# Probability times values in head pairs: values as the stationary operand, two heads side by side in one PSUM bank, rows no longer transposed a second time

## Chip, core and metric

One NeuronCore of one Trainium2 chip runs the whole program. The metric is the device time of one execution in microseconds (us). The engines are TensorE (PE, and PEld for its weight loads), VectorE (DVE), ScalarE (ACT), GpSimd (POOL) and SyncE (SP, which issues most transfers).

## The reference

Six transformer layers for 256 tokens of width 1024. The change touches the softmax attention in five of them. With `h` heads of 64 features, each head computes

```python
sc = jnp.einsum('bkgqd,bksd->bkgqs', qg, k) * scale        # (+ bias, window or causal mask)
o = jnp.einsum('bkgqs,bksd->bkgqd', jax.nn.softmax(sc, axis=-1), v)
mix = jnp.concatenate([merge_heads(a_out), merge_heads(b_out), merge_heads(c_out), merge_heads(d_out)], axis=-1)
mix = jnp.einsum('bse,ed->bsd', mix, w_o[l])
```

- Two layers of the first block (called MIX here) have 20 softmax items each: 8 of differential attention, which come in pairs that are subtracted from one another and then normalised, and 12 plain ones (4 grouped-query, 4 neighbourhood, 4 latent heads), not causal: 256 queries by 256 keys.
- Two layers of the second block (SWA, with a sink logit and a window) and one (FOX, with a forget gate) have 16 plain, causal items each. The fourth (GLA) has no softmax.

So there are 16 items of the differential kind and 24 + 32 + 16 = 72 plain ones.

## The kernel before

Weights come in units of 128 x 2048 through three buffers `raw`. ACT rounds each into `whi` (`act_hi`, L885), DVE makes the rest `wlo` (`dve_lo`, L894), and each product is three matmuls (hi x hi, hi x lo, lo x hi). These matmuls fill nearly all the time of PE.

Attention is laid into slots between quarters of such units, by the tables `MIX`, `SWA` and `FOX` of class `Plan`. In each slot every engine does, in its own fixed order, a part of several items. An item k whose scores are made in slot h is transposed in slot h+2 and valued in slot h+3.

- PE: a quarter of a unit; transposes of the probabilities of an item into bank `pso` (L737), scores (L751); then `pe_value` (L766); then, where the table has a turn, `pe_turn` (L612). In slots where the plan is `joint`, the scores of two heads stand together in the even slot: their 64 features lie in the upper and the lower half of the partitions, and their results go to two banks.
- ACT: the copy of the transposed probabilities to `probT` (L796), the exponentials with their row sums (L810), the rounding of a turned column block to `ahi` (L645), and `act_hi`.
- DVE: the masked scores and their maxima (L846 or L840), then `dve_divide` (L819 to L828), then `alo` (L649), then other work of the slot, such as rotary embeddings, `dve_lo`, and products for the modulation.

An item's output is tokens by features: `probT` is stationary (128 x 128), the 64 value features move, and there are 4 matmuls of 64 columns, or 3 if causal. DVE divides by the row sums and writes 128 x 64 blocks into `rows`. The output projection wants features by tokens, so when two heads are ready, `pe_turn` transposes their 128 columns back and ACT and DVE split them into `ahi` and `alo`.

The semaphores that order it are `s_done` (scores), `max_ready`, `p_ready` (exponentials), `t_done` (transposes), `pt_ready` (copy), `o_done` (values), `o_evac` (divided). `prob` has two buffers, and the mask of item k waits for the transposes of item k-2, since both use one of them.

Of the kernel before, what the change touches and what calls it, by code (L numbers as in the profile page):

```python
# [113 lines left out]
def build(nc, wts, ada, ada_b, x_in, c_row, rel_bias, col1, row1, gain_mix, gain_ffn, col2, row2,  # L114
# [4 lines left out]
    with ctx:  # L119
# [77 lines left out]
        prob, probT = fold(w(8000, 1024), 2, 512), fold(w(9024, 1024), 2, 512)  # L197
# [62 lines left out]
        o_evac = sem("o_evac")  # L260
        mix_ready = sem("mix_ready")
# [345 lines left out]
        def pe_turn(pe, g, m, bank=1):  # L607

            if not isinstance(m, int) or m > 0:
                pe.wait_ge(m_lo, 8 * g + m)  # L610
# [29 lines left out]
        def act_turn(act, l, c, m, g, bank=1):  # L640

            act.wait_ge(m_tr, 8 * g + m + 1)
            if m >= 4:
                act.wait_ge(unit_mm, unit_no(l, c) + m // 2 - 1)
            nc.scalar.copy(ahi[:, m % 4], psu[:, bank, 0:SEQ]).then_inc(m_hi, 1)  # L645

        def dve_turn(dve, m, g, bank=1):
            dve.wait_ge(m_hi, 8 * g + m + 1)
            nc.vector.tensor_tensor(alo[:, m % 4], psu[:, bank, 0:SEQ], ahi[:, m % 4].bitcast(f32), ALU.subtract).then_inc(m_lo, 1)  # L649
# [77 lines left out]

        def pe_begin(pe, I0, items, plan, h):
# [3 lines left out]
            if k is not None:  # L732
                pe.wait_ge(p_ready, I0 + k + 1)
                if k >= 1:
                    pe.wait_ge(pt_ready, I0 + k)
                for _, _, at in blocks(items[k]):
                    last = nc.tensor.transpose(pso[:, at:at + P], prob[:, k % 2, at:at + P], ident[:])  # L737
# [18 lines left out]
        def pe_value(pe, I0, items, plan, h):  # L756
            k = plan.value(h)
            if k is not None:
                it = items[k]
                pe.wait_ge(pt_ready, I0 + k + 1)  # L760
                if k >= 1:
                    pe.wait_ge(o_evac, I0 + k)
                if it["vpre"] is not None:
                    pe.wait_ge(*it["vpre"])
                for t, kc, at in blocks(it):
                    last = mm(psm[:, t * HD:(t + 1) * HD], probT[:, k % 2, at:at + P],  # L766
                              it["v"][kc], start=(kc == 0), stop=(kc == 1 or at == P))
                last.then_inc(o_done, 1)

        def pe_mix_turn(pe, I0, plan, h, g):  # L770


            m = plan.turn.get(h)
            if m is not None:
                pe.wait_ge(o_evac, I0 + 2 * m + 2)
                pe_turn(pe, g, m)

        def pe_mix1_turn(pe, l, I0, h):
# [3 lines left out]
            if m is not None:  # L782
                if m < 2:
                    pe.wait_ge(mix_ready, l + 1)
                else:
                    pe.wait_ge(o_evac, I0 + 2 * m + 6)
                pe_turn(pe, l, m)

        def act_copy(act, I0, items, plan, h):
            k = plan.transpose(h)  # L790
            if k is not None:
                act.wait_ge(t_done, I0 + k + 1)
                if k >= 2:
                    act.wait_ge(o_done, I0 + k - 1)
# [1541 lines left out]
```

## Time and profile before

| | |
|---|---|
| median of 3 runs | 1897.2 us (1896.7 to 1898.39) |
| the profiled execution: its time, its span | 1897.12 us, 1895.1 us |
| PE, PEld, DVE, ACT, POOL busy, share of the span | 98%, 90%, 71%, 50%, 4% |
| granted clock of TensorE, mean | 0.998 |
| all value matmuls (L766), x608 records, busy | 80.9 us |
| all transposes of probabilities (L737), x304, busy | 47.6 us |
| all transposes of rows (L612), x96, busy | 18.7 us |
| exponentials (L810), x144, busy with their form's mean 463 ns | 66.5 us |

Each float32 matmul shows as two records, a transpose and an fp32r matmul as one. Records of matmuls overlap, so the time that a group takes is read from its start to the start of the group behind it, not from the sum of the durations. Windows are in us from the start of the span. The attention stages lie at 56 to 135 and 386 to 465 (MIX), 698 to 762 and 1631 to 1695 (SWA) and 1322 to 1408 (FOX).

### The profile page before, as it was taken

How to read it: one execution, taken by the hardware profiler on the slowest of the kernel's cores; microseconds unless marked ns; L12 is line 12 of the kernel's file. 1: busy time of each engine (PE TensorE's matmuls, PEld its weight loads, DVE VectorE, ACT ScalarE, POOL GpSimd, SP SyncE). 2: the span in 40 equal slices, each digit the busy share in tenths (PEclk: the TensorE clock that was granted, in tenths of full speed). 3: DMA queues.
4: the chain of work that ended last, by engine and by line, in shares of the span. 5: the costliest groups of instructions: out<-in, count | busy, mean ns of one | idle time of the engine just before them, and what ended most of it. 6: DMA issues, size and time to landing. Idle time of an engine off the chain costs nothing.

```text
span 1895.1 us, 34211 instructions
## 1 busy us (share of the span) xinstructions
PE 1855.8 (98%) x13368; PEld 1702.6 (90%) x13368; DVE 1354.9 (71%) x2194; ACT 953.2 (50%) x1470; POOL 77.0 (4%) x98
## 2 busy tenths in 40 slices
PE   8999999999999999999999999999999999999998
PEld 8989999998999987899989799998989998979997
DVE  6758888775878877888877587886555556766555
ACT  7755334766533466533473553345654334664333
POOL 3003000000000000000000000003300000000000
PEclk9999999999999999999999999999999999999999
DMA  8538987533788742788854388875335554335552
GB/s 305 188 125 259 353 307 304 190 134 134 290 329 307 297 177 97 262 326 308 315 198 139 119 300 323 306 279 225 122 138 190 192 181 165 132 113 199 189 187 89
DMA packets 62060, 416.60 MB, mean 220 GB/s; under 512 B 9008, under 2 KB 9200, under 8 KB 13312
## 3 DMA queue, kind: packets, MB, share of 16 engines
q1 hardware_dynamic: 56016, 401.33, 57.4%
q0 software_dynamic: 5936, 13.79, 2.6%
q8 instruction: 72, 1.18, 0.2%
q14 instruction: 36, 0.29, 0.0%
HBM read 413.90 MB, written 3.19 MB: 220 GB/s over the span
## 4 chain that ended last, share of the span: by engine, by line
PE 89%; DVE 6%; ACT 2%; issue 1%; DVEq 1%; ACTq 0%; DMA 0%; SPq 0%
PE psu L524 35%; PE psy L692 18%; PE psy L586 7%; PE psy L578 5%; PE psy L632 5%; PE psu L541 4%; PE psm L766 3%; PE psy L565 2%; PE psu L751 2%; PE pso L737 1%; PE psy L655 1%; DVE x L1164 1%; DVE wlo L894 1%; PE psy L1680 1%; DVEq L1163 1%
## 5 line engine op out<-in xcount | busy, mean ns | idle before, releaser
L885 ACT CAST whi<-raw 128x2048 fp32r<-128x2048 f32 (+1 forms) x281 | 536.2, 1908 | 599.1 <-PE psu L524 396.4
L894 DVE TENSOR_TENSOR wlo<-raw,whi 128x2048 fp32r<-128x2048 f32 (+5 forms) x306 | 646.6, 2114 | 257.2 <-ACT whi L885 256.5
L524 PE MATMUL psu<-hlo,whi 128*128 128x256 f32 x1920 | 536.0, 279 | 0.0
L524 PE MATMUL psu<-hhi,whi 128*128 128x256 f32 x1920 | 535.9, 279 | 0.0
L524 PE MATMUL psu<-hhi,wlo 128*128 128x256 f32 x1920 | 535.8, 279 | 0.0
L524 PEld LDWEIGHTS psu<-hhi,whi 128*128 128x128 f32 x1920 | 360.8, 188 | 2.3
L524 PEld LDWEIGHTS psu<-hlo,whi 128*128 128x128 f32 x1920 | 360.8, 188 | 2.3
L524 PEld LDWEIGHTS psu<-hhi,wlo 128*128 128x128 f32 x1920 | 360.8, 188 | 0.0
L1096 DVE CUSTOM_DVE_ANT_0 ada_raw<-ada_raw,cvec 128x1024 f32<-128x1024 f32 x192 | 227.0, 1220 | 2.2 <-DMA ada_raw<-ada 2.2
L692 PE MATMUL psy<-whi,ahi 128*128 128x512 f32 x528 | 210.2, 398 | 0.0
L692 PE MATMUL psy<-wlo,ahi 128*128 128x512 f32 x528 | 207.9, 394 | 0.0
L692 PE MATMUL psy<-whi,alo 128*128 128x512 f32 x528 | 207.4, 393 | 0.0
L586 PE MATMUL psy<-whi,hhi 128*128 128x256 f32 x448 | 131.4, 293 | 0.0
L586 PE MATMUL psy<-wlo,hhi 128*128 128x256 f32 x448 | 125.9, 281 | 0.0
L586 PE MATMUL psy<-whi,hlo 128*128 128x256 f32 x448 | 125.8, 281 | 0.0
L692 PEld LDWEIGHTS psy<-wlo,ahi 128*128 128x128 f32 x528 | 99.1, 188 | 25.4
L692 PEld LDWEIGHTS psy<-whi,alo 128*128 128x128 f32 x528 | 99.1, 188 | 21.0
L692 PEld LDWEIGHTS psy<-whi,ahi 128*128 128x128 f32 x528 | 99.1, 188 | 20.5
L586 PEld LDWEIGHTS psy<-whi,hhi 128*128 128x128 f32 x448 | 84.5, 189 | 4.9 <-issue 4.8
L766 PEld LDWEIGHTS psm<-work 128*128 128x128 f32 x608 | 76.1, 191 | 13.5 <-issue 7.2
L810 ACT ACTIVATE work<-work,nmax 128x256 f32<-128x256 f32 (+1 forms) x144 | 66.5, 463 | 40.9 <-DVE nmax L846 40.9
L586 PEld LDWEIGHTS psy<-whi,hlo 128*128 128x128 f32 x448 | 84.6, 189 | 0.1
(337 smaller groups left out, 2981.2 us busy)
## 6 DMA issues: line engine op xcount, KB each, us to landing
raw<-wts SPq DMA_DIRECT2D x280, 1024.0 KB, 4.8
ada_raw<-ada SPq DMA_DIRECT2D x96, 1024.0 KB, 5.0
gain<-gate_rows POOLq DMA_DIRECT2D x8, 512.0 KB, 3.9
dense_bias<-rel_bias POOLq DMA_DIRECT2D x32, 64.0 KB, 10.1
nab<-dense_bias SPq DMA_DIRECT2D x2, 1024.0 KB, 7.1
ada_raw<-fox_rows POOLq DMA_DIRECT2D x4, 512.0 KB, 13.3
cb<-cst POOLq DMA_DIRECT2D x1, 1408.0 KB, 8.2
cb<-cst SPq DMA_DIRECT2D x1, 1056.0 KB, 10.1
```

Of the source, the lines that this page charges most:

```text
L524: last = mm(psu[:, bank, cc * SEQ:(cc + 1) * SEQ], a[:, cols], h[:, kt, :], start=(kt == 0 and j == 0), stop=(kt == KT - 1 and j == 2))
L541: last = mm(psu[:, banks[u], cc * SEQ:(cc + 1) * SEQ], a[:, cols], h[:, kt, :], start=(kt == 0 and cc == 0 and j == 0), stop=(kt == KT - 1 ...
L565: last = mm(psy[:, j, half * width:(half + 1) * width], h[:, kt, toks], a[:, kt * width:(kt + 1) * width], start=start, stop=stop, skip_gr ...
L578: last = mm(o, a[:, cols], h[:, kt, :], start=(kt == 0 and j == 0), stop=(kt == KT - 1 and j == 2))
L586: last = mm(o, h[:, kt, toks], a[:, kt * width:(kt + 1) * width], start=(kt == 0 and j == 0), stop=(kt == KT - 1 and j == 2))
L632: last = mm(psy[:, 2 * t + half, :], h[:, (2 * s + ff) % 4, toks], b[:, cols], start=(s == 0 and ff == 0 and j == 0), stop=(s == 3 and ff ...
L692: last = mm(psy[:, 2 * t + half, :], h[:, aslot + ff, toks], b[:, cols], start=(first_step and ff == 0 and j == 0), stop=(last_step and ff ...
L766: last = mm(psm[:, t * HD:(t + 1) * HD], probT[:, k % 2, at:at + P], it["v"][kc], start=(kc == 0), stop=(kc == 1 or at == P))
L810: last = nc.scalar.activation(prob[:, k % 2, span], src[:, span], ACT.Exp, bias=nmax[:, k % 4, t:t + 1], scale=1.0 if plain else -1.0, acc ...
L885: nc.scalar.copy(whi[:, part_of(c), 0:n], raw[:, slot_of(c), 0:n]).then_inc(hi_done, 1)
L894: last = nc.vector.tensor_tensor(wlo[:, part_of(c), cols], raw[:, slot_of(c), cols], whi[:, part_of(c), cols].bitcast(f32), ALU.subtract)
L1096: last = nc.vector.tensor_tensor_reduce(tile, tile, cvec[:], 1.0, 0.0, ALU.mult, ALU.add, ada_part[:, 2 * half + j:2 * half + j + 1])
```

## The change

The 16 differential items stay as they are. For the 72 plain items:

- The exponentials are normalised before the transposes. DVE makes the reciprocals one slot after the scores (`dve_roots`, first in its slot), and ACT multiplies the probabilities in place, two activations per item (`act_normal`, between the copy and the exponentials of a slot). The transposes wait for that (`pn_ready`) instead of for the exponentials.
- Nothing is valued at the even item. At the odd one, the values of both heads are stationary (128 x 64 each) and `probT` moves, 256 columns at a time. The two heads' results lie in partitions 0 to 63 and 64 to 127 of one bank, features by tokens. `probT` gets a third buffer, and its two key halves are laid so that a head's 256 queries lie in one row.
- DVE copies the 128 x 256 result once per pair (`dve_divide`), and ACT and DVE make `ahi` and `alo` from the copy. `pe_turn` stays only for the differential heads (two per MIX layer) and for GLA.

```diff
-        prob, probT = fold(w(8000, 1024), 2, 512), fold(w(9024, 1024), 2, 512)
+        prob, probT = fold(w(8000, 1024), 2, 512), fold(w(9024, 1536), 3, 512)
...
             if k is not None:
-                pe.wait_ge(p_ready, I0 + k + 1)
+                if items[k]["pair"] is None:
+                    pe.wait_ge(pn_ready, plain_no(I0, items, k) + 1)
+                else:
+                    pe.wait_ge(p_ready, I0 + k + 1)
                 if k >= 1:
                     pe.wait_ge(pt_ready, I0 + k)
...
                 it = items[k]
+                if it["pair"] is None and k % 2 == 0:
+                    return
                 pe.wait_ge(pt_ready, I0 + k + 1)
...
+                if it["pair"] is None:
+                    for kc in range(2):
+                        for i in (k - 1, k):
+                            toks, at = (slice(kc * P, SEQ), P + kc * SEQ) if it["causal"] else (slice(0, SEQ), kc * SEQ)
+                            last = mm(psm[HD * (i % 2):HD * (i % 2) + HD, toks], items[i]["v"][kc],
+                                      probT[:, i % 3, at:at + toks.stop - toks.start], start=(kc == 0), stop=(kc == 1))
+                    last.then_inc(o_done, 2)
+                    return
...
+        def act_normal(act, I0, items, plan, h):
+            k = plan.score(h - 1)
+            if k is not None and items[k]["pair"] is None:
+                act.wait_ge(r_ready, plain_no(I0, items, k) + 1)
+                for t, span in enumerate(spans(items[k])):
+                    last = nc.scalar.activation(prob[:, k % 2, span], prob[:, k % 2, span], ACT.Copy, scale=rsum[:, k % 4, t:t + 1])
+                last.then_inc(pn_ready, 1)
+
+        def dve_roots(dve, I0, items, plan, h):
+            k = plan.score(h - 1)
+            if k is not None and items[k]["pair"] is None:
+                dve.wait_ge(p_ready, I0 + k + 1)
+                if items[k]["sink"] is not None:
+                    nc.vector.tensor_tensor(psum_[:, k % 4], psum_[:, k % 4], esink[:, k % 4], ALU.add)
+                    nc.vector.drain()
+                nc.vector.reciprocal(rsum[:, k % 4], psum_[:, k % 4]).then_inc(r_ready, 1)
...
+            if it["pair"] is None:
+                if k % 2 == 1:
+                    dve.wait_ge(o_done, I0 + k + 1)
+                    m = k // 2 - (2 if plan is MIX else 0)
+                    nc.vector.tensor_copy(columns(plan, m), psm[:, 0:SEQ]).then_inc(o_evac, 2)
+                return
...
-                pe_mix_turn(pe, I0, SWA, h, g)
...
                 act_copy(act, I0, items, SWA, h)
+                act_normal(act, I0, items, SWA, h)
...
-                    act_turn(act, DEPTH1, c0 + 6, SWA.turn[h], g)
+                    m = SWA.turn[h]
+                    act_turn(act, DEPTH1, c0 + 6, m, g, columns(SWA, m), o_evac, I0 + 2 * m + 2)
```

On PE, in an SWA layer where a slot takes one quarter of the output projection (L632, in the new program L634), from the end of one slot to the end of the next. Before:

```order
L766 MATMUL psm<-work 128x64 x3
L612 MATMUL psu<-ident,rows 128x128 x2
L632 MATMUL psy<-whi,ahi 128x512
L632 MATMUL psy<-whi,alo 128x512
L632 MATMUL psy<-wlo,ahi 128x512
L632 MATMUL psy<-whi,ahi 128x512
L632 MATMUL psy<-whi,alo 128x512
L632 MATMUL psy<-wlo,ahi 128x512
L737 MATMUL pso<-ident,work 128x128 x3
L751 MATMUL psu<-work 128x128
L751 MATMUL psu<-work 128x256
L766 MATMUL psm<-work 128x64 x3
```

Now, the same place (L759 are the transposes, L773 the scores, L793 the values):

```order
L759 MATMUL pso<-ident,work 128x128 x3
L634 MATMUL psy<-whi,ahi 128x512
L634 MATMUL psy<-whi,alo 128x512
L634 MATMUL psy<-wlo,ahi 128x512
L634 MATMUL psy<-whi,ahi 128x512
L634 MATMUL psy<-whi,alo 128x512
L634 MATMUL psy<-wlo,ahi 128x512
L759 MATMUL pso<-ident,work 128x128 x3
L773 MATMUL psu<-work 128x128
L773 MATMUL psu<-work 128x256
L793 MATMUL psm<-work 64x256 x2
L793 MATMUL psm<-work 64x128 x2
```

The two groups of three narrow matmuls and the two transposes of rows are gone, and four wider ones stand at the end of every second slot, each with 64 output partitions.

On ACT, one slot of an SWA layer that holds an evacuation (L1742), a column block to round (L645) and a weight unit (L885). Before:

```order
L1742 ACTIVATE work<-psy 128x512
L796 COPY work<-pso 128x384
L808 ACTIVATE esink<-nmax,prow 128x2
L810 ACTIVATE work,psum_<-work,nmax 128x128
L810 ACTIVATE work,psum_<-work,nmax 128x256
L645 CAST ahi<-psu 128x256
L885 CAST whi<-raw 128x2048
```

Now:

```order
L1794 ACTIVATE work<-psy 128x512
L817 COPY work<-pso 128x384
L843 ACTIVATE work<-work,rsum 128x128
L843 ACTIVATE work<-work,rsum 128x256
L829 ACTIVATE esink<-nmax,prow 128x2
L831 ACTIVATE work,psum_<-work,nmax 128x128
L831 ACTIVATE work,psum_<-work,nmax 128x256
L647 CAST ahi<-rows 128x256
L934 CAST whi<-raw 128x2048
```

Two activations have come in ahead of the exponentials, and the rounding reads SBUF instead of PSUM.

On DVE, a slot with an odd item in the joint part of an SWA layer. Before:

```order
L846 ISA work,nmax<-psy,cb,nsink 128x128
L846 ISA nmax 128x1
L846 ISA work,nmax<-psy,cb,nsink 128x256
L846 ISA nmax 128x1
L819 TENSOR_TENSOR psum_<-psum_,esink 128x2
L821 RECIPROCAL rsum<-psum_ 128x2
L828 TENSOR_TENSOR rows<-psm,rsum 128x2x64
L649 TENSOR_TENSOR alo<-psu,ahi 128x256
L894 TENSOR_TENSOR wlo<-raw,whi 128x1024
```

Now:

```order
L853 TENSOR_TENSOR psum_<-psum_,esink 128x2
L855 RECIPROCAL rsum<-psum_ 128x2
L893 ISA work,nmax<-psy,cb,nsink 128x128
L893 ISA nmax 128x1
L893 ISA work,nmax<-psy,cb,nsink 128x256
L893 ISA nmax 128x1
L651 TENSOR_TENSOR alo<-rows,ahi 128x256
L943 TENSOR_TENSOR wlo<-raw,whi 128x1024
```

The sum and the reciprocal moved ahead of the mask, where they wait for ACT's exponentials of the slot before; the division is gone.

## Rows read from the trace of the kernel before

**Rows 1.** The page: busy time by engine; the chain that ended last, by engine.

```profile
PE 1855.8 (98%) x13368; PEld 1702.6 (90%) x13368; DVE 1354.9 (71%) x2194; ACT 953.2 (50%) x1470; POOL 77.0 (4%) x98
...
PE 89%; DVE 6%; ACT 2%; issue 1%; DVEq 1%; ACTq 0%; DMA 0%; SPq 0%
```

**Rows 2.** Busy time in windows of four slots: two of SWA, one of MIX.

```profile
core 0: us, PE busy (x) PEld busy (x) DVE busy (x) ACT busy (x) POOL busy (x), PEclk, DMA share, GB/s
1641.99:1654.66 12.67, 12.67 (x111) 11.60 (x110) 7.86 (x33) 9.46 (x29) 0.00 (x0) 1.00 0.20 77
1654.66:1668.42 13.76, 13.21 (x89) 10.56 (x88) 10.53 (x37) 9.48 (x29) 0.00 (x0) 1.00 0.21 77
101.13:116.63 15.50, 15.50 (x95) 12.89 (x93) 9.14 (x27) 8.96 (x25) 0.00 (x0) 1.00 0.28 101
```

**Rows 3.** Timeline of PE in MIX: start, length, engine, line, operation, count.

```profile
92.11 1.00 PE L766 MATMUL psm<-work 128*128 128x64 f32 x8
92.92 0.36 PE L586 MATMUL psy<-whi,hhi 128*128 128x256 f32 x1
...
94.97 0.48 PE L751 MATMUL psu<-work 64*128 64x256 f32 x1
94.97 0.48 PE L751 MATMUL psy<-work 64*128 64x256 f32 x1
...
96.03 1.10 PE L766 MATMUL psm<-work 128*128 128x64 f32 x8
96.97 0.39 PE L612 MATMUL psu<-ident,rows 128*128 128x128 f32 x2
```

**Rows 4.** Timeline of PE in SWA: slots 10 and 11.

```profile
1640.45 0.37 PE L751 MATMUL psu<-work 64*128 64x128 f32 x1
...
1641.30 0.88 PE L766 MATMUL psm<-work 128*128 128x64 f32 x6
1641.99 0.36 PE L586 MATMUL psy<-whi,hhi 128*128 128x256 f32 x1
...
1643.83 0.78 PE L766 MATMUL psm<-work 128*128 128x64 f32 x6
1644.45 0.39 PE L612 MATMUL psu<-ident,rows 128*128 128x128 f32 x2
1644.59 0.36 PE L586 MATMUL psy<-whi,hhi 128*128 128x256 f32 x1
```

**Rows 5.** Timeline of PE in FOX: values after a quarter.

```profile
1343.23 0.78 PE L766 MATMUL psm<-work 128*128 128x64 f32 x6
1343.82 0.37 PE L578 MATMUL psy<-hhi,whi 128*128 128x256 f32 x1
```

**Rows 6.** Timeline of ACT in SWA, slot 10 and the copy of slot 11.

```profile
1642.20 0.30 ACT L808 ACTIVATE esink<-nmax,prow 128x2 f32<-128x2 f32 x1 [1.17 <-DVE nmax L846]
1642.40 0.39 ACT L810 ACTIVATE work<-work,nmax 128x128 f32<-128x128 f32 x1
1642.70 0.19 ACT L810 ACTIVATION_READ_ACCUMULATOR work<-work,nmax 128x1 f32 x1
1642.79 0.49 ACT L810 ACTIVATE work<-work,nmax 128x256 f32<-128x256 f32 x1
1643.19 0.19 ACT L810 ACTIVATION_READ_ACCUMULATOR work<-work,nmax 128x1 f32 x1
...
1644.19 0.47 ACT L796 COPY work<-pso 128x384 f32<-128x384 f32 x1
```

**Rows 7.** Timeline of DVE in SWA, slot 10.

```profile
1641.40 0.35 DVE L846 CUSTOM_DVE_ANT_0 work<-psu,cb,nsink 128x128 f32<-128x128 f32 x1 [0.59 <-PE psy L751]
...
1642.22 0.16 DVE L819 TENSOR_TENSOR psum_<-psum_,esink 128x2 f32<-128x2 f32 x1
1642.46 0.17 DVE L821 RECIPROCAL rsum<-psum_ 128x2 f32<-128x2 f32 x1
```

**Rows 8.** The longest kind of wait in SWA, 1631 to 1695: us in total, times, longest.

```profile
ACT esink L808 <- DVE nmax L846: 12.6, 10, 2.0
```

More of the change, by code:

```diff
@@ L726, in blocks, with turned_at, columns, plain_no @@
                 (t, kc, t * SEQ + kc * P) for t in range(NT) for kc in range(2)]
+        def turned_at(it, t, kc, at):
+            return at if it["causal"] or it["pair"] is not None else kc * SEQ + t * P
+        def columns(plan, m):
+            at = 256 if plan is MIX and m == 4 else m * SEQ
+            return scratch[:, at:at + SEQ]
+        def plain_no(I0, items, k):
+            before = sum(it["pair"] is None for it in items[:k])
+            return I0 - 8 * min(I0 // 20, DEPTH1) + before
         def pe_begin(pe, I0, items, plan, h):
@@ L732, in pe_begin @@
             if k is not None:
-                pe.wait_ge(p_ready, I0 + k + 1)
+                if items[k]["pair"] is None:
+                    pe.wait_ge(pn_ready, plain_no(I0, items, k) + 1)
+                else:
+                    pe.wait_ge(p_ready, I0 + k + 1)
                 if k >= 1:
                     pe.wait_ge(pt_ready, I0 + k)
-                for _, _, at in blocks(items[k]):
-                    last = nc.tensor.transpose(pso[:, at:at + P], prob[:, k % 2, at:at + P], ident[:])
+                for t, kc, at in blocks(items[k]):
+                    to = turned_at(items[k], t, kc, at)
+                    last = nc.tensor.transpose(pso[:, to:to + P], prob[:, k % 2, at:at + P], ident[:])
                 last.then_inc(t_done, 1)
@@ L869, in dve_steps @@
             if h in plan.turn:
-                dve_turn(dve, plan.turn[h], g)
+                m = plan.turn[h]
+                dve_turn(dve, m, g, psu[:, 1, 0:SEQ] if plan is MIX and m < 2 else columns(plan, m))
         def act_hi(act, l, c, i=0, first=False):
@@ L1329, in act_mix1 @@
                 act_copy(act, I0, items, MIX, h)
+                act_normal(act, I0, items, MIX, h)
                 act_exp(act, I0, items, MIX, h)
@@ L1374, in act_mix1 @@
                 if h in MIX.turn:
-                    act_turn(act, l, C1_O, MIX.turn[h], l)
+                    m = MIX.turn[h]
+                    if m < 2:
+                        act_turn(act, l, C1_O, m, l, psu[:, 1, 0:SEQ], m_tr, 2 * l + m + 1)
+                    else:
+                        act_turn(act, l, C1_O, m, l, columns(MIX, m), o_evac, I0 + 2 * m + 6)
                 if h == 33:
@@ L1775, in act_fox @@
                 act_copy(act, I0, items, FOX, h)
+                act_normal(act, I0, items, FOX, h)
                 act_exp(act, I0, items, FOX, h)
@@ L1788, in act_fox @@
                 if h in FOX.turn:
-                    act_turn(act, DEPTH1, c0 + 13, FOX.turn[h], g)
+                    m = FOX.turn[h]
+                    act_turn(act, DEPTH1, c0 + 13, m, g, columns(FOX, m), o_evac, I0 + 2 * m + 2)
                 if h == 28:
@@ L1883, in act_gla @@
                 if h in GLA.turn:
-                    act_turn(act, DEPTH1, c0 + 13, GLA.turn[h], g, 0)
+                    act_turn(act, DEPTH1, c0 + 13, GLA.turn[h], g, psu[:, 0, 0:SEQ], m_tr, 2 * DEPTH1 + GLA.turn[h] + 1)
                 if h == 57:
@@ L1990, in dve_gla @@
                 if h in GLA.turn:
-                    dve_turn(dve, GLA.turn[h], g, 0)
+                    dve_turn(dve, GLA.turn[h], g, psu[:, 0, 0:SEQ])
                 if h in (4, 40):
```

48 lines of the change are left out of this document (20 added, 28 removed).

## The prediction

> **What bounds the kernel now.** I read the page first: PE is busy for 98% of the span and holds 89% of the chain that ended last, DVE 71% and 6%, ACT 50% and 2% [rows 1]. So a microsecond taken out of PE's stream comes out of the time, as long as another engine does not take its place. Whether one does is not told by a mean over the span, so I then read windows of four slots inside the stages that change [rows 2]. PE is busy nearly throughout at the full granted clock (1.00, the 2.4 GHz level) in all three. ACT is busy 9.46 of 12.67 us in the first half of SWA, 9.48 of 13.76 in the second, 8.96 of 15.50 in MIX; DVE 7.86, 10.53 and 9.14. That is the room into which the change puts work. Last I read PE's timeline for what a value group takes, from its start to the next group's [rows 3 to 5].
>
> **What leaves PE.** A value group of a plain item in MIX takes 92.92 - 92.11 = 0.81 us alone, and 96.97 - 96.03 = 0.94 right behind scores [rows 3]. In SWA it takes 1641.99 - 1641.30 = 0.69 behind scores and 1644.45 - 1643.83 = 0.62 otherwise, and the two transposes of rows behind it 0.14 [rows 4]. In FOX it takes 1343.82 - 1343.23 = 0.59 [rows 5]. Two items and one turn make a pair: 0.94 + 0.81 + 0.14 = 1.89 us in MIX, 0.69 + 0.62 + 0.14 = 1.45 in SWA, 0.59 + 0.59 + 0.14 = 1.32 in FOX.
>
> **What comes into PE.** No row shows a matmul with 64 output partitions beside another. The nearest rows are the joint scores: two heads in two halves of the array, by rows of the array instead of by columns. Their records in `psu` and `psy` start together at 94.97, and the whole of them (per half four records of 256 columns) takes 96.03 - 94.97 = 1.06 us [rows 3]. The causal form (per half two records of 128 columns and two of 256) takes 1641.30 - 1640.45 = 0.85 [rows 4]. The new value group has the same records per half: two key blocks, each float32 and so two records, of 256 columns without a mask, of 256 and 128 with it. If its halves run side by side, it takes 1.06 and 0.85. These prices hold the cost of leaving the split array, and 28 of the 36 groups stand in slots with scores or late in their stage, mostly right behind scores, where the array was split already (by rows, not by columns: no row shows what that change costs, and I take nothing, with 0.1 apiece, 2.8 us, as the other end). In FOX a quarter lies between, so I add the 0.1 by which a group changed in length beside a split one (0.94 against 0.81) [rows 3]: 0.95.
>
> If the halves run one after the other, the streaming comes twice. The two forms differ by 2 x 128 columns and by 1.06 - 0.85 = 0.21 us, so a record of 256 columns streams for 0.21, four of them for 0.84 and the causal four for 0.63; the rest, 0.22, is switching. A group then takes 1.90 and 1.48, and 1.58 in FOX. These are the two ends. I take the first, since the nearest row has two halves of this same array side by side in float32 at just this length.
>
> - MIX: 6 pairs in each of 2 layers, 12 x (1.89 - 1.06) = 10.0 us less.
> - SWA: 8 pairs in each of 2 layers, 16 x (1.45 - 0.85) = 9.6 us less.
> - FOX: 8 pairs, 8 x (1.32 - 0.95) = 3.0 us less.
>
> Together 22.6 us, if nothing else holds PE.
>
> **What comes into ACT.** Two activations per plain item. An activation of this kind, SBUF to SBUF with a scale per partition, is nearest to the exponentials: 1642.70 - 1642.40 = 0.30 us for 128 columns and 1643.19 - 1642.79 = 0.40 for 256 [rows 6]. So an SWA or FOX item costs 0.70 and a MIX item 0.80 (bounds: 0.39 and 0.49 apiece if nothing overlaps). ACT loses nothing; the rounding to `ahi` only reads another place. Four slots then ask of ACT [rows 2]:
>
> - SWA, first half: 9.46 + 4 x 0.70 = 12.26 us, where PE wants 12.67 - 2 x 0.60 = 11.47. ACT is now the longer one.
> - SWA, second half: 9.48 + 2.80 = 12.28, where PE wants 13.76 - 1.20 = 12.56. ACT fills 98% of it.
> - MIX: 8.96 + 4 x 0.80 = 12.16, where PE wants 15.50 - 2 x 0.83 = 13.84: 88%.
>
> This is where gain is given back. In the first half of SWA (three pairs) I count all of it as lost, 3 x 0.60 = 1.8 us a layer: 0.8 a window by the sums above, and the rest because ACT's load comes in lumps (weight units) and it waits for DVE, 12.6 us in ten waits in the last SWA stage [rows 8], not all of which can go. In the second half I count half of three pairs, 0.9; the last two pairs, behind the last scores, keep all. That is 2.7 a layer, 5.4 us for both. For MIX I take 0.5 a layer, 1.0 together, for FOX nothing.
>
> **The new ring.** DVE's reciprocals now stand first in its slot and wait for the exponentials of the slot before; mask and maxima stand behind them, and ACT's next exponentials wait for these. Round the ring: the exponentials with their sums 1643.19 + 0.19 - 1642.20 = 1.18 us [rows 6], sum and start of the reciprocal some 0.3, mask and maxima from 1641.40 until ACT starts at 1642.20, 0.80 [rows 6, 7]. That is 2.3 us, with hand-overs 2.4, for a slot of 12.67 / 4 = 3.2 (2.9 after the change). So the ring alone does not bind. Behind the blocked reciprocal on DVE are the mask, the copy of values, the rest `alo` that the output projection waits for, and `dve_lo`, which PE's next weight unit waits for; a half-unit of `dve_lo` in the slot ahead makes the reciprocal late, then the normalising, then PE's transposes. Between one slot's transposes and the next's, ACT needs only copy and normalising, 0.4 + 0.7, so some 1.8 us of lateness are free.
>
> **What leaves DVE.** A pair had two divisions and now has one copy of 128 x 256. The two turns of `psu` on PE no longer wait for DVE. DVE gets no longer in any window, and where it is busiest (10.53 of 13.76) it is not the longest. I count nothing.
>
> **Sum.** 1897.1 (the profiled execution, whose span is 1895.1, and which lies 0.1 from the median) - 22.6 + 5.4 + 1.0 = 1880.9. The two givings-back are the least certain, and lean to more rather than less: I say 1882.
>
> **The rivals.** A measurement of this kernel can tell about 0.2%, 3.8 us, from no change.
>
> 1. *Side by side, a part given back in SWA* (forecast, 0.71): 1874 to 1889. At the low end ACT's work is absorbed everywhere (22.6 less), at the high end SWA gains nothing and MIX gives back 3.
> 2. *The halves run one after the other* (0.13). The joint scores differ in that each half reads other rows of the array; here both halves take all 128 rows, and two streams must enter at once. What would decide it is that the second head's matmuls start when the first's end. Then MIX gets 12 x (1.89 - 1.90) = -0.1 us, SWA 16 x (1.45 - 1.48) = -0.5, FOX 8 x (1.32 - 1.58) = -2.1: 2.7 longer. With the 2.8 for the change from a row split to a column split it is 1897.1 + 5.5 = 1903, slower. PE is then long enough to hide ACT.
>    The Trainium skill, "TensorE: Matmul & The Clock Gate", Part 3, says that weight loads run beside matmuls in flight only where the row groups differ, which here they don't; by it each load would stand bare between the matmuls. By that rule this rival would hold. The trace does not agree for the full array: the eight loads and matmuls of a value group, all in the same row group, take 0.81 us [rows 3]. The same part says that three column tiles gained 2.38 times, which speaks for the first case; no run here shows it yet.
> 3. *ACT and DVE set the pace of all the stages* (0.16). Speaking for it: 98% and over 100% in SWA, and the ring. Against it: 88% in MIX. If each slot of SWA's 14 with scores or transposes became 0.5 us longer than PE wants, by DVE's other work falling into the ring, that is 14 us for both layers; with 2 in MIX and 1 in FOX it leaves 22.6 - 17 = 5.6: 1891.5, from 1888 to 1899.
>
> **How the numbers follow.** The time is that of the first case. Faster by over 0.2% (under 1893.4): the first case and over a third of the third, 0.77. Within 0.2%: the rest of the third and a little of the second, 0.11. Slower: 0.12. The range leaves out less than a tenth below 1874 and over a tenth above 1898; the first case's own is 1874 to 1889.
>
> **What would show it.** Side by side: the records of L793 start in twos, and a group takes 1.06 or 0.85. The normalising: L843 at 0.30 and 0.40 apiece. In SWA: ACT over 95% busy from slot 9 to 19, and PE's transposes (L759) idle ahead for ACT, by 0.5 to 1 us after each weight unit; in MIX and FOX hardly. Wrong would make it: a value group near 1.9 (second case), PE idle in every slot, or an activation with a scale per partition that costs more than the exponentials.

## The result and the profile after

The changed kernel takes 1914.4 us (median of 4 runs, 1910.9 to 1915.14) against 1897.5 us before (4 runs beside it, 1896.7 to 1898.39). The ratio is 1.0086, 95% interval [1.007, 1.0102]: slower, by less than 1% but clear of the noise. The forecast was 1882.0 us, from 1874 to 1898. The profiled execution took 1915.1 us, its span is 1913.4.

The page of the changed kernel, busy time by engine and the chain by engine, against [rows 1]:

```profile
PE 1845.7 (96%) x13104; PEld 1665.3 (87%) x13104; DVE 1346.5 (70%) x2158; ACT 1006.6 (53%) x1614; POOL 78.1 (4%) x98
...
PE 84%; DVE 7%; ACT 5%; issue 2%; DVEq 1%; ACTq 1%; DMA 0%; SPq 0%
```

PE works 10.1 us less, and yet the span is 18.3 us longer. PE no longer works without a break: its part of the chain fell from 89% to 84%, and ACT's rose from 2% to 5%. To see where, read the five attention stages as windows, in the order MIX, MIX, SWA, FOX, SWA, each from its normalisation to the start of the feed-forward part behind it. Before:

```profile
core 0: us, PE busy (x) PEld busy (x) DVE busy (x) ACT busy (x) POOL busy (x), PEclk, DMA share, GB/s
8.30:146.10 137.80, 136.51 (x1006) 123.66 (x1004) 95.36 (x208) 96.49 (x204) 16.56 (x22) 1.00 0.58 200
338.90:476.40 137.50, 135.74 (x1005) 122.52 (x1005) 92.58 (x207) 90.81 (x200) 0.61 (x2) 1.00 0.38 142
669.30:765.40 96.10, 93.70 (x660) 81.95 (x660) 70.74 (x186) 61.60 (x150) 2.25 (x5) 0.98 0.37 131
1283.20:1411.30 128.10, 124.91 (x954) 114.05 (x954) 72.43 (x150) 74.78 (x148) 32.73 (x27) 1.00 0.44 161
1602.40:1697.80 95.40, 92.00 (x661) 80.59 (x661) 67.27 (x179) 63.01 (x153) 1.07 (x2) 1.00 0.33 116
```

And after:

```profile
8.20:149.80 141.60, 134.35 (x945) 115.74 (x943) 93.69 (x202) 106.16 (x228) 16.57 (x22) 0.99 0.56 195
342.60:484.20 141.60, 133.53 (x945) 114.48 (x945) 91.03 (x201) 100.51 (x224) 0.65 (x2) 0.99 0.37 138
677.00:781.30 104.30, 94.02 (x612) 76.07 (x612) 69.84 (x178) 73.28 (x182) 2.29 (x5) 0.93 0.34 123
1299.00:1423.10 124.10, 120.81 (x906) 106.12 (x906) 69.75 (x142) 85.83 (x180) 33.78 (x27) 1.00 0.46 166
1614.30:1716.00 101.70, 90.08 (x612) 73.08 (x612) 66.08 (x171) 74.30 (x185) 1.07 (x2) 0.98 0.31 109
```

These windows hold the whole difference. Their lengths sum to 594.9 us before and 613.3 after, 18.4 more; FOX is 4.0 shorter, MIX 7.9 longer in two layers, SWA 14.5 longer in two. Three terms make this up:

- Length less PE's busy time is PE's idle time: 12.1 us before, 40.5 after, **28.5 more**. FOX has none of it (3.2 and 3.3).
- A stage's length times what its mean granted clock lacks of 1.00 is at most what the clock took: 1.4 + 1.4 + 7.3 + 2.0 = 12.1 us after, 1.9 before, **up to 10 more**.
- What is left, 18.4 - 28.5 - 10.2 = **-20.3 us**, is the work that left PE's stream, if the clock took all of that. The forecast was 22.6.

So matmul work left PE's stream about as forecast, and nearly twice of it was given back. Who holds PE is seen in the group of the transposes over the whole program (idle time ahead of it behind the second bar; it was 0.1 us before the change):

```profile
L759 PE MATMUL pso<-ident,work 128*128 128x128 f32 x304 | 49.7, 280 | 20.6 <-ACT work L843 20.5
```

And in the waits of the last SWA stage, 1640 to 1712 (us in total, times, longest):

```profile
DVE alo L651 <- ACT ahi L647: 12.4, 7, 2.2
ACT work L843 <- DVE rsum L855: 8.2, 7, 1.6
PEld pso L759 <- ACT work L843: 7.8, 10, 1.6
PE pso L759 <- ACT work L843: 5.2, 7, 1.2
```

PE waits for ACT's normalising, ACT for DVE's reciprocal, and DVE, ahead of that reciprocal, for ACT's rounding `ahi`. One turn of this ring, on the timeline of the same stage, DVE first, then ACT, then PE:

```profile
1667.44 0.43 DVE L651 TENSOR_TENSOR alo<-rows,ahi 128x256 fp32r<-128x256 f32 x1 [1.76 <-ACT ahi L647]
1667.78 1.22 DVE L943 TENSOR_TENSOR wlo<-raw,whi 128x1024 fp32r<-128x1024 f32 x1
1668.91 0.15 DVE L853 TENSOR_TENSOR psum_<-psum_,esink 128x2 f32<-128x2 f32 x1
1669.14 0.17 DVE L855 RECIPROCAL rsum<-psum_ 128x2 f32<-128x2 f32 x1
```

```profile
1666.92 0.19 ACT L831 ACTIVATION_READ_ACCUMULATOR work<-work,nmax 128x1 f32 x1
1667.01 0.39 ACT L647 CAST ahi<-rows 128x256 fp32r<-128x256 f32 x1
1667.30 0.47 ACT L817 COPY work<-pso 128x384 f32<-128x384 f32 x1
1669.34 0.80 ACT L843 ACTIVATE work<-work,rsum 128x128 f32<-128x128 f32 x2 [1.56 <-DVE rsum L855]
```

```profile
1669.64 0.28 PE L588 MATMUL psy<-wlo,hhi 128*128 128x256 f32 x1
1670.20 0.55 PE L759 MATMUL pso<-ident,work 128*128 128x128 f32 x3 [0.28 <-ACT work L843]
```

The exponentials and their sums are done at 1667.11. The reciprocal needs 0.17 us and starts at 1669.14, two microseconds later: DVE sat 1.76 us for `ahi`, which ACT makes behind the same exponentials, and then did 1.22 us of a weight unit. ACT idles 1.56 us, and the transposes start late; PE had other work to do meanwhile and idles only 0.28 us. No engine is short of time here; each waits for a small piece that stands behind another engine's large one. Where PE has less work left to cover the lateness, it idles longer. In MIX two products of 1.22 us stand ahead of the reciprocal (L1145, from 85.14 on), and PE idles 0.86 us:

```profile
87.69 0.15 DVE L855 RECIPROCAL rsum<-psum_ 128x2 f32<-128x2 f32 x1
87.88 0.91 ACT L843 ACTIVATE work<-work,rsum 128x256 f32<-128x256 f32 x2 [1.54 <-DVE rsum L855]
88.84 0.66 PE L759 MATMUL pso<-ident,work 128*128 128x128 f32 x4 [0.86 <-ACT work L843]
```

There is a second way from the reciprocal to PE, through what stands behind it on DVE. The reciprocal, and in SWA the sum ahead of it, wait for ACT's exponentials, so the mask of the next item comes late. In each SWA stage one projection quarter is to write into `psy` where the last joint scores stand, and waits until the mask has read them. The longest idle time of PE in the stage comes so, the sum on DVE first:

```profile
1679.64 0.16 DVE L853 TENSOR_TENSOR psum_<-psum_,esink 128x2 f32<-128x2 f32 x1 [1.38 <-ACT work L831]
1680.29 0.48 DVE L893 CUSTOM_DVE_ANT_0 work<-psy,cb,nsink 128x256 f32<-128x256 f32 x1
1680.92 0.77 PE L634 MATMUL psy<-whi,ahi 128*128 128x512 f32 x1 [2.26 <-DVE nmax L893]
```

Over the program the first matmuls of all these quarters (L634) have 7.3 us of idle time ahead of them, 4.5 of it for the mask; the same group (L632) had 1.2 us before.

In the four slots that the prediction took as its SWA example, first and second half [rows 2]:

```profile
1654.46:1668.24 13.78, 12.01 (x99) 9.53 (x97) 7.21 (x29) 11.72 (x36) 0.00 (x0) 1.00 0.19 73
1668.24:1685.95 17.71, 13.64 (x76) 9.52 (x75) 11.47 (x41) 13.08 (x39) 0.00 (x0) 0.90 0.17 61
```

The first took 12.67 before and now 13.78, the second 13.76 and now 17.71. ACT is busy for 85% and 74%, not for over 95%.

The new value group does what was forecast, and a little more. In MIX (98.51 to the turn at 99.52) it takes 1.01 us, in FOX and SWA 0.80; the estimates were 1.06, 0.95 and 0.85:

```profile
98.51 1.08 PE L793 MATMUL psm<-work 128*64 128x256 f32 x8
99.52 0.44 PE L614 MATMUL psu<-ident,rows 128*128 128x128 f32 x2
...
1349.62 0.87 PE L793 MATMUL psm<-work 128*64 128x256 f32 x8
1350.42 0.39 PE L580 MATMUL psy<-hhi,whi 128*128 128x256 f32 x1
```

### The profile page after: what moved, and what is told of

Read it like the earlier page. It is cut to its first block, busy times and chain, and to the rows that moved or that the text cites. A ratio compares the mean times of both kernels' runs of the same rounds, so it can differ in the third digit from the quotient of the medians.

```text
span 1913.4 us, 33683 instructions
## 1 busy us (share of the span) xinstructions
PE 1845.7 (96%) x13104; PEld 1665.3 (87%) x13104; DVE 1346.5 (70%) x2158; ACT 1006.6 (53%) x1614; POOL 78.1 (4%) x98
## 4 chain that ended last, share of the span: by engine, by line
PE 84%; DVE 7%; ACT 5%; issue 2%; DVEq 1%; ACTq 1%; DMA 0%; SPq 0%
PE psu L526 35%; PE psy L694 18%; PE psy L588 6%; PE psy L580 5%; PE psy L634 5%; PE psu L543 4%; PE psy L567 2%; PE psu L773 2%; ACT work L831 2%; PE psy L657 1%; DVE wlo L943 1%; DVE x L1213 1%; PE pso L759 1%; ACT work L843 1%; PE psm L793 1%
## 5 line engine op out<-in xcount | busy, mean ns | idle before, releaser
L1145 DVE CUSTOM_DVE_ANT_0 ada_raw<-ada_raw,cvec 128x1024 f32<-128x1024 f32 x192 | 226.9, 1219 | 2.5 <-DMA ada_raw<-ada 2.5
L694 PE MATMUL psy<-whi,ahi 128*128 128x512 f32 x528 | 210.0, 398 | 0.0
L694 PEld LDWEIGHTS psy<-whi,ahi 128*128 128x128 f32 x528 | 99.1, 188 | 20.6
L634 PE MATMUL psy<-whi,ahi 128*128 128x512 f32 x192 | 84.2, 438 | 7.3 <-DVE nmax L893 4.5
L588 PEld LDWEIGHTS psy<-wlo,hhi 128*128 128x128 f32 x448 | 84.4, 188 | 0.0
## 6 DMA issues: line engine op xcount, KB each, us to landing
dense_bias<-rel_bias POOLq DMA_DIRECT2D x32, 64.0 KB, 10.2
```

Of the source, the lines that this page charges most:

```text
L588: last = mm(o, h[:, kt, toks], a[:, kt * width:(kt + 1) * width], start=(kt == 0 and j == 0), stop=(kt == KT - 1 and j == 2))
L634: last = mm(psy[:, 2 * t + half, :], h[:, (2 * s + ff) % 4, toks], b[:, cols], start=(s == 0 and ff == 0 and j == 0), stop=(s == 3 and ff ...
L694: last = mm(psy[:, 2 * t + half, :], h[:, aslot + ff, toks], b[:, cols], start=(first_step and ff == 0 and j == 0), stop=(last_step and ff ...
L1145: last = nc.vector.tensor_tensor_reduce(tile, tile, cvec[:], 1.0, 0.0, ALU.mult, ALU.add, ada_part[:, 2 * half + j:2 * half + j + 1])
```

## The experiments

Three theories were open. *The ring*: PE waits for the chain of exponentials, reciprocal (DVE) and normalising (ACT). Its first rival: ACT's added 53 us of work alone make it the bound. Its second: the saved matmuls themselves did not come, or came by another mechanism than the two column halves. All times below stand beside runs of the kernel before of 1897.2 to 1897.5 us on the same chip.

**1. No ring at all.** The last line goes in MIX and in FOX in the same way.

```diff
-                if items[k]["pair"] is None:
-                    pe.wait_ge(pn_ready, plain_no(I0, items, k) + 1)
-                else:
-                    pe.wait_ge(p_ready, I0 + k + 1)
+                pe.wait_ge(p_ready, I0 + k + 1)
...
-            dve_roots(dve, I0, items, plan, h)
...
-                act_normal(act, I0, items, SWA, h)
```

> The changed kernel without the normalising: no reciprocals for the plain items on VectorE, no normalising activations on ScalarE, and the transposes wait for the exponentials as before. The plain heads' results are left undivided. What is left of the change is TensorE's part and the single copy per pair. Theory A (the new step reciprocal - normalising - transposes, with VectorE's other work of a slot in it, makes TensorE wait and its clock fall): all of the loss goes and TensorE's saving shows, 1873 to 1880 us, granted clock 0.998 as before. Theory B (the new value groups or the later copies cost TensorE more than the sum says): it stays above 1895 us.

Measured: 1883.2 us (1882.53 to 1884.28), ratio 0.9927 [0.9911, 0.9944]. The stages are 136.4, 134.4, 93.2, 124.2 and 92.7 us, 14.0 less than before; with 22.2 us of idle time against 12.1 and a clock that lacks 1.4 us instead of 1.9, the same sum gives 23.6 us for the work that left the stream. The plain heads' results stay undivided here. The new form without its normalising is worth 14.3 us, 3 less than even the low end of what was expected (the time was to be 1880 at most): PE idles 10.1 us more than before the change though the ring is gone. In MIX the turn of the differential heads waits 4.9 us for DVE's `alo` (0.8 before), in SWA the projection quarters (L634) idle 4.4 us (0.6 before). The 31.2 us up to the changed kernel come with the normalising and its ring.

**2. ACT's part of the ring alone.** Same work on ACT, but by a column of ones, waiting only for its own exponentials; no reciprocals on DVE, and so undivided results again.

```diff
-                act.wait_ge(r_ready, plain_no(I0, items, k) + 1)
+                act.wait_ge(p_ready, I0 + k + 1)
...
-                    last = nc.scalar.activation(prob[:, k % 2, span], prob[:, k % 2, span], ACT.Copy, scale=rsum[:, k % 4, t:t + 1])
+                    last = nc.scalar.activation(prob[:, k % 2, span], prob[:, k % 2, span], ACT.Copy, scale=ones[:, 0:1])
...
-            dve_roots(dve, I0, items, plan, h)
```

> The changed kernel in which ScalarE normalises by a column of ones, waiting only for its own exponentials, and VectorE makes no reciprocals for the plain items: ScalarE has all the added work and the transposes wait for it, but VectorE is out of the loop. The plain heads' results are left undivided. Theory A (VectorE's queue in the loop): most of the loss goes, 1878 to 1888 us. Theory C (my forecast's: ScalarE's added load sets the pace in SWA): the loss in SWA stays, 1900 to 1914 us in all, with ScalarE over 95% busy in the first half of SWA.

Measured: 1894.8 us (1892.02 to 1895.68), ratio 0.9982 [0.9972, 0.9991], between the two expectations. The transposes' group now shows

```profile
L759 PE MATMUL pso<-ident,work 128*128 128x128 f32 x304 | 48.7, 276 | 6.1 <-ACT work L843 5.8
```

ACT's normalising costs 1894.8 - 1883.2 = 11.6 us, the reciprocals on DVE another 1914.4 - 1894.8 = 19.6. DVE's part is the larger one, though it is one instruction of 0.15 to 0.17 us per item, and one more in SWA. The 19.6 us hold three things that this pair of kernels does not separate: ACT waits for the reciprocal, DVE waits for the exponentials ahead of it and is late with what stands behind, and DVE is busy 13.2 us longer over the whole program (1346.5 against 1333.3).

**3. The reciprocals earlier on DVE.** They move from the head of the next slot to the tail of their own, behind the division and ahead of the long pieces:

```diff
-            dve_roots(dve, I0, items, plan, h)
             k = plan.value(h)
...
+            dve_roots(dve, I0, items, plan, h + 1)
             if h in plan.turn:
```

> The changed kernel, complete, with VectorE's reciprocals moved from the start of the next slot to the same slot as the scores, behind the copy of values and ahead of the turned block's rest, the rotary work and the weight units. VectorE then waits there for the exponentials, but none of its long pieces stands between them and the reciprocal. Theory A: most of the loss goes, 1880 to 1892 us. Theory C: nothing changes, 1908 to 1918 us. Theory D (VectorE's waiting for the exponentials delays its own weight units instead): 1895 to 1915 us, with waits of TensorE for wlo in place of those for the normalising.

Measured: 1911.5 us (1909.56 to 1915.89), ratio 1.0079 [1.0063, 1.0096]. The transposes' idle time falls from 20.6 to 9.6 us, and the two MIX stages take 138.1 and 137.7 us, as before the change. ACT's wait for the reciprocal is all but gone (39.5 us in the changed kernel, 2.4 here). But DVE now stands still for ACT's exponentials in nearly every slot, 72.6 us in 63 waits against 16.3 in 16, and its mask is late instead. In the last SWA stage:

```profile
1674.96 0.16 DVE L853 TENSOR_TENSOR psum_<-psum_,esink 128x2 f32<-128x2 f32 x1 [1.42 <-ACT work L831]
1676.25 0.76 PE L634 MATMUL psy<-whi,ahi 128*128 128x512 f32 x1 [2.68 <-DVE nmax L893]
```

That stage takes 104.5 us instead of 101.7, FOX 126.5 instead of 124.1. The time lies in the ranges of both Theory C and Theory D. It is D's mechanism with another end: what PE waits for is the mask and not `wlo`. The wait was moved, not removed.

**4. The same, and ACT's normalising ahead of its copy.**

```diff
-                act_copy(act, I0, items, SWA, h)
                 act_normal(act, I0, items, SWA, h)
+                act_copy(act, I0, items, SWA, h)
```

> As the kernel with early reciprocals, and on ScalarE the normalising stands ahead of the copy in each slot, so that it needn't wait for the slot's transposes. Theory A: as e3 or up to 3 us less. If the copy that now comes 0.7 to 0.8 us later holds up the value groups, it is up to 4 us more than e3.

Measured: 1914.7 us (1913.94 to 1915.77), ratio 1.0093 [1.0076, 1.011]. No better than experiment 3, whose runs overlap with these: the transposes now wait 11.8 us for ACT's copy in place of its normalising.

**5. The reciprocals on GpSimd.** Its queue is empty in MIX and in SWA's attention.

```diff
-            if k is not None and items[k]["pair"] is None:
+            if plan is FOX and k is not None and items[k]["pair"] is None:
...
+                pool.wait_ge(p_ready, I0 + k + 1)
...
+                nc.gpsimd.tensor_tensor(rsum[:, k % 4], psum_[:, k % 4], minus1[:], ALU.pow).then_inc(r_ready, 1)
```

> The changed kernel with the reciprocals of the MIX and SWA heads on GpSimd, whose queue is idle there (as a power of minus one), and only FOX's on DVE. The whole computation is done. Theory (about 20 of the 31 us that the new ring costs come from the reciprocal standing in DVE's queue behind its long pieces): near the kernel whose ACT waits for its own exponentials alone, 1894.8, plus GpSimd's latency: 1893 to 1900 us, with hardly any wait of ACT for the reciprocal that a DVE piece ends. Rival (any further engine in the ring costs a hop that PE cannot afford, and DVE's queue has little to do with it): 1905 to 1915 us.

Measured: 1897.8 us (1896.99 to 1903.32), ratio 1.0002 [0.9992, 1.0011]. This takes back 16.6 of the 19.6 us that hang on the reciprocals, with the whole computation done. GpSimd is slow at it, but no long piece stands ahead:

```profile
1650.56 0.20 POOL L452 TENSOR_TENSOR psum_<-psum_,esink 128x2 f32<-128x2 f32 x1 [1.98 <-ACT work L771]
1650.90 0.89 POOL L454 TENSOR_TENSOR rsum<-psum_,minus 128x2 f32<-128x2 f32 x1
```

Sum and power take 0.20 and 0.69 to 0.89 us where DVE takes 0.15 and 0.17 (spans on this engine are rough). The Trainium skill, "Perfetto Trace Analysis", on optimizing GPSIMD operations, advises to prefer other engines because GpSimd is generally slower. On the operation the trace agrees, four to five times (though a power stands here against a reciprocal); on the kernel it does not: the slower engine gives the shorter time. The profiled execution is the longest of the ten, 1903.3 us, 5.5 above the median, so it shows less than the whole gain. ACT waits 23.9 us for reciprocals in it instead of 39.5, and the transposes idle

```profile
L699 PE MATMUL pso<-ident,work 128*128 128x128 f32 x304 | 49.8, 280 | 15.0 <-ACT work L783 14.8
```

instead of 20.6. The gain stands in MIX, where these idle times fall from 10.0 us to 1.6 in the two layers. In the two SWA layers they rise from 10.5 to 13.4, and the stages take 101.7 and 102.1 us against 104.3 and 101.7. So in this execution a queue of its own for the reciprocals does not free SWA; whether it does in the faster ones, no trace shows.

**6. The ring without the saving.** The kernel before, with reciprocals first in the slot, normalising on ACT and the transposes waiting for it; the divisions become copies.

```diff
-                pe.wait_ge(p_ready, I0 + k + 1)
+                if items[k]["pair"] is None:
+                    pe.wait_ge(pn_ready, plain_no(I0, items, k) + 1)
+                else:
+                    pe.wait_ge(p_ready, I0 + k + 1)
...
+            if it["pair"] is None:
+                nc.vector.tensor_copy(rows[:, :, it["col"]:it["col"] + HD], fold(psm[:, 0:P], NT, HD)).then_inc(o_evac, 1)
+                return
```

> The kernel before with the new ring alone: DVE makes the reciprocals first in the slot after the scores, ACT normalises in place, PE's transposes wait for that, and DVE's division of each plain head becomes a copy of the 128x128 result. PE does the same work as before. The whole computation is done. Theory (the ring itself costs what the profile after shows as idle PE, about 27 us of idle and up to 10 us of halved clock, whatever PE does besides): about 1897 + 25 to 35 = 1922 to 1932 us, with the SWA stages and the MIX stages longer by 5 to 9 us each and idle time before the transposes. Rival (PE waits only since its own stream became shorter; with the old stream of 22 us more the same chain fits): below 1907 us.

Measured: 1918.2 us (1917.23 to 1918.86), ratio 1.0106 [1.0091, 1.0122]: 20.9 us more than before. It lies outside both expectations, nearer to the theory's. The stages are 141.9, 141.7, 103.1, 129.0 and 100.5. So the normalising and its ring cost 20.9 us even where PE has all its old work to cover them, and some 10 more (31.2) where it does not. DVE is not busier here than before the change (1349.9 us against 1354.9, since the divisions became copies), so the loss is not a matter of DVE's total work.

**7. FOX alone in the new form.** The windows of after say that only FOX gained.

```diff
-                if it["pair"] is None and k % 2 == 0:
+                if it["new"] and k % 2 == 0:
```

(and so in the six other places that ask for `pair`; only FOX's items carry `new`.)

> The new path is kept in the FOX stage alone (8 pairs of heads); the MIX and SWA stages go back to the kernel before. The whole computation is done. Theory (the loss is a wait on the chain of DVE's reciprocal, ACT's normalising and PE's transposes, which two quarters of the projection per slot cover in FOX and one per slot does not elsewhere): the FOX stage keeps its 124 us against 128 before, its PE idle time stays at about 2 us, every other stage reads as before (137.7, 96, 95.5), and the total is 1893.6 us, ratio 0.998. Rival (FOX's gain depends on something in the stages ahead, or is bought by the slower clock elsewhere): the FOX stage reads 126 us or more, or another stage moves by over 1 us, and the total lies at 1896 or above.

Measured: 1893.65 us (1892.66 to 1894.64, 11 runs), ratio 0.9978 [0.9969, 0.9987]: the whole computation, faster than both kernels, and as expected. FOX takes 124.3 us, the other stages 137.6, 137.5, 96.1 and 95.4.

**8. Which mechanism makes the value group short.** First another order of the four matmuls, heads outside and key blocks inside, on the kernel of experiment 1:

```diff
-                    for kc in range(2):
-                        for i in (k - 1, k):
+                    for i in (k - 1, k):
+                        for kc in range(2):
```

> The changed kernel with no reciprocals and no normalising for the plain heads (they are left undivided), and with PE's four value matmuls of a pair in another order: both key blocks of the even head, then both of the odd head, where the changed kernel alternates the heads. To be compared with the same kernel in alternating order, 1883.2 us. Theory (two heads' matmuls into column halves of the array run side by side only when they alternate): a group of four takes 1.9 us in MIX and 1.5 in the causal stages instead of 1.01 and 0.80, 36 pairs lose 0.7 to 0.9 us each, and the total is 1883 + 25 to 30 = 1908 to 1913 us. Rival (the group is short because each matmul with 64 output partitions is short by itself, in any order): groups stay at 1.0 and 0.8 us, total 1883 us. Between: only the middle pair of the four overlaps, groups 1.45 and 1.15, total about 1896 us.

Measured: 1883.6 us (1883.01 to 1884.68). Nothing changes, as the rival said; a group takes 1.02 us. But that rival's reason was not yet shown, so the next kernel keeps this order and puts both results into the same half of the array:

```diff
-                            last = mm(psm[HD * (i % 2):HD * (i % 2) + HD, toks], items[i]["v"][kc],
+                            last = mm(psm[0:HD, SEQ * (i % 2) + toks.start:SEQ * (i % 2) + toks.stop], items[i]["v"][kc],
```

> As the run with the heads apart (no reciprocals, no normalising, both key blocks of one head and then of the other), but with both heads' results in partitions 0 to 63, in columns 0 to 255 and 256 to 511 of the bank. The copy behind it still reads 128 partitions of the first 256 columns. So no two of the four matmuls of a pair can lie in different column halves of the array. Theory (the eight records of a group start in four pairs because the two heads occupy the two column halves, in whatever order they are written): the pairs are gone, a group takes about 1.8 us in MIX and 1.4 in the causal stages, and the total is 1883.5 + 20 to 28 = 1904 to 1912 us. Rival (a matmul with 64 output partitions is recorded as two that start together, wherever its result goes): groups stay at 1.02 and 0.80 us and the total at 1883 to 1885 us.

Measured: 1901.8 us (1901.34 to 1902.49), 18.1 more, a little under the 20 to 28 of the theory, and a group in MIX takes 1.87 us:

```profile
95.57 1.94 PE L790 MATMUL psm<-work 128*64 128x256 f32 x8
97.44 0.44 PE L614 MATMUL psu<-ident,rows 128*128 128x128 f32 x2
```

So it is the two column halves, and the rival of a matmul that is short by itself falls.

**9. Scores ahead of transposes on PE,** to give the ring more time; then with the normalising ahead of ACT's copy as well. In `pe_begin` the two blocks change places.

```diff
-            k = plan.transpose(h)
...
-                last.then_inc(t_done, 1)
             k = plan.score(h)
...
+            k = plan.transpose(h)
...
+                last.then_inc(t_done, 1)
```

> The changed kernel with PE's transposes behind the scores of the slot instead of ahead of them; nothing else moves, and the whole computation is done. The transposes then come 0.4 to 1.1 us later on PE, and the mask and the exponentials can start that much earlier. Theory (PE waits because the chain from one slot's exponentials over DVE's reciprocal and ACT's normalising to the transposes is late by 0.5 to 1.5 us where one quarter of the projection covers it): some half of the 28 us of new idle time goes, 1900 to 1908 us. Rival (the chain is a ring through ACT's copy behind the transposes, so that moving the transposes moves the copy and the normalising with them): 1911 to 1920 us.

> As the run before, and on ACT the normalising stands ahead of the copy of the transposed block, so that the ring does not go through that copy; the whole computation is done. Theory: less idle time than in either single edit, 1896 to 1905 us. Rival (what is late is the reciprocal behind DVE's long pieces, and ACT now stands waiting for it ahead of its copy too): 1908 to 1918 us.

Measured: 1918.2 us (1915.03 to 1919.92), ratio 1.0105 [1.0088, 1.0122], and 1923.7 us (1921.57 to 1927.28), ratio 1.0135 [1.0118, 1.0152]. Both miss the theory's range. The first lies in its rival's, the second above it. In the second, ACT's wait for the reciprocal in the last SWA stage grew from 8.2 us to

```profile
ACT work L843 <- DVE rsum L855: 14.7, 11, 1.9
```

## Why the prediction was wrong

**Where the 32.4 us of the miss lie.** 8.3 are the part of the 22.6 that does not reach the time even without the ring (14.3 do, experiment 1), 5.2 are what ACT's normalising costs above the 6.4 allowed for it (11.6, experiment 2), and 19.6 are the reciprocals, for which the sum had nothing. (The forecast was rounded up by 1.1, and the kernel before measured 0.4 more.)

**What leaves and enters PE: right.** -22.6 us was the term; the windows of after give -20.3 and those of experiment 1 -23.6, and experiment 8 shows the mechanism by taking it away. The ends for the halves one after the other (1.90 and 1.48 us) were right too: the same half takes 1.87 in MIX and 1.45 in SWA (1645.15 to 1646.60). FOX was 3.0 and is 4.0: a group there takes 0.80 and not 0.95, so what I had added for leaving the split array behind a quarter does not show. What was wrong is the condition behind the term, "if nothing else holds PE": PE idles 10.1 us more in experiment 1. The rule that I weighed against it (the Trainium skill, "TensorE: Matmul & The Clock Gate", Part 3, on weight loads only beside other row groups) did not hold here either: all eight loads are of the same row group, and the group takes 1.01 us. That part's gain for column tiles, 2.38 times with three, agrees in kind: 1.87 / 1.02 = 1.83 with two.

**What comes into ACT: the work was right, its consequence wrong.** Two activations take 0.80 us in SWA and 0.91 in MIX; 0.70 and 0.80 were said. But I gave gain back where ACT's busy time exceeded PE's. ACT's busy time rises by 53.4 us and stays at 85% of the tightest window. The sum of busy times gave 5.4 + 1.0 us for something that, by experiments 1 and 2, costs 11.6; its place in the chain, which that sum does not see, is the likely reason.

**"So the ring alone does not bind ... some 1.8 us of lateness are free": this step failed.** The round of 2.4 us for a slot of 2.9 was added up from operations that follow each other at once. On DVE they do not: the reciprocal stands behind what the slot before put last, up to 2.1 to 2.4 us of rope, mask table, products or weight unit, and behind a wait of up to 2.5 us for `ahi`. I named the half unit of `dve_lo` and put it against the 1.8 free, as if it came alone. And I did not carry on from the blocked reciprocal to PE through the mask behind it, though I named the order. The experiments give this step 19.6 us (with the reciprocals against without), 16.6 of them given back by a queue of its own.

**"What leaves DVE ... I count nothing": half right.** DVE's busy time falls by 8.0 us in the windows. What counts is the order: the old reciprocal stood at the division and nobody but the division needed it; the new one has ACT, and behind it PE, waiting.

**The clock was not in the sum.** The term for it was nothing, without a reason given. Ahead of the longest stretch at 1.2 GHz in SWA, PE had been busy for 7.15 of 10.07 us; in the same part of the stage before the change, 725.5 to 745.5, it was busy for 9.6 to 9.7 of 10 us and stayed at 2.4 GHz. After:

```profile
732.00:742.07 10.07, 7.15 (x43) 4.55 (x42) 6.67 (x23) 9.15 (x28) 0.00 (x0) 1.00 0.32 104
742.07:752.31 10.24, 9.08 (x27) 6.22 (x28) 5.87 (x17) 4.75 (x17) 0.00 (x0) 0.50 0.00 0
```

The second row holds 27 records of matmuls, the first 43, in the same time. If the idle time is what made the clock fall, which these rows suggest and no run tried alone, it had a surcharge here of up to a third (10 on 28.5 us).

**The chances.** The case that came true is a worse form of the third rival, ACT and DVE setting the pace. It put 14 us into SWA and 2 into MIX. By the windows, with my terms for the saving, it is 14.5 + 9.6 = 24.1 and 7.9 + 10.0 = 17.9. It got 0.16, and its high end, 1899, let the loss exceed the saving by 2 us, where it did by 17. Of what I said would show it, the waits of the transposes behind ACT are there in SWA, but in MIX just the same, and ACT is not full.

**Not settled.** How ACT's 11.6 us divide between its work and the two more hand-overs, how the 19.6 divide between the late reciprocal, the late mask and the reciprocals' own time on DVE, and which of DVE's long pieces costs most, was not tried. None of the four orders of these queues that were tried wins SWA back; whether one does is open.

## What to carry to other kernels

When a step moves from behind a matmul to ahead of it, do not weigh its length against the engine's free time; follow the semaphore: which engine must do a tiny operation, what is the longest piece in that queue ahead of it, what stands behind it while it waits, and does the reader of either result hold PE. Here the stage with two projection quarters per slot (FOX) hid the ring and the stages with one did not (that this is the reason is argued, not tried), so try the change stage by stage: here one stage gives 3.6 us, and all together lose 17. If a tiny operation must sit in a ring, an idle engine that is four times slower at it can be the better place.

## What the runs showed of the hardware

In these kernels two float32 matmuls with 64 output partitions each, into different column halves, run side by side even when they are not written next to each other. In the kernel with the heads apart the program order of a causal pair is 256, 128 (even head), 256, 128 (odd head), two records each. Its records in a window of 0.5 us around the start of such a group (1629.45 to 1629.95), and below them those of the kernel with both in the same half, which has the same order, in 0.72 us (1645.12 to 1645.84):

```profile
L790 PE MATMUL psm<-work 128*64 128x256 f32 x4 | 0.7, 404 | 0.0
```

```profile
L790 PE MATMUL psm<-work 128*64 128x256 f32 x2 | 0.6, 404 | 0.0
L790 PE MATMUL psm<-work 128*64 128x128 f32 x2 | 0.4, 272 | 0.0
```

With two halves, four records of 256 columns have begun and none of 128, though only two of the four can be the even head's: the odd head's first matmul has passed the even head's second. With one half, two of 256 and two of 128 have begun, which is the program order. The Trainium skill, "TensorE: Matmul & The Clock Gate", Part 2, says that matmuls stay in program order and only weight loads are pulled ahead; for two column halves this trace does not agree.
